# Nine conditioning pairs of a hybrid encoder summed on VectorE ahead of TensorE, with two more weight slots

## Chip, cores and metric

One core of one Trainium2 chip runs the whole kernel in one launch. The metric is the device time of that core in microseconds, the median of several executions. The reference's output, in float32, is what the kernel must produce.

## What is computed

Two groups of tokens, a prompt of 512 and a sample of 64, pass through a trunk of two layers at width 1024. Every layer takes a condition vector per group and turns it into 6 x 1024 values (a shift, a gain and a gate for each of two blocks):

```
mod = silu(c) @ ada_w[l] + ada_b[l]            # (2 groups, 6 * 1024)
sh1, sc1, g1, sh2, sc2, g2 = split(mod, 6)
xm = rms(x) * (1 + sc1) + sh1                  # first block's input
q, k, v, o, gates = split(xm @ w_in)           # mLSTM mixer of layer 0
...
x = x + g1 * (h @ w_out)                       # h from the matrix memory, gated by sigmoid(o)
xm = rms(x) * (1 + sc2) + sh2
x = x + g2 * swiglu(xm)
```

Layer 1 has differential attention in the mixer's place. The 6 x 1024 values of layer 0 are 48 units of 128; the first 16 (shift and gain of the first block) are needed at the very start, the other 32 (units 16 to 47) form 16 pairs, numbered 0 to 15. None of the pairs is needed before the gate and the second block of layer 0.

## The kernel before

Tensors lie feature by token: 8 tiles (k = 0 to 7) of 128 features by 576 tokens. A weight matrix is cut in units of 128 output features, one unit being 8 tiles of 128 x 128, that is 512 KB. SyncE's queue loads units in a fixed, written-out order into two raw slots (`load_unit`, L431); GpSimd splits each into a high and a low part (`split_unit`, L613 and L617) as soon as TensorE has left the slot's parts; TensorE multiplies high by high, high by low and low by high (`project`, L730: 48 matmuls of 288 columns a unit; `project_values`, L786: 28 matmuls of 512 columns a unit for V). The units of the mixer are the gates (0), Q (1 to 4), K (5 to 8), V (9 to 16), O (17 to 24) and the output matrix (25 to 32). The kernel calls a matvec of a conditioning pair `modulate(p)`. It stands in TensorE's instruction stream between units: one after unit 2 and one after each two units of Q and K (p = 0 to 3), one after each two units of V (p = 4 to 7), one inside the matrix-memory core at every odd head (p = 8 to 11) and one after each two units of the output matrix (p = 12 to 15).

A matvec (L741) has silu(c) spread over 32 columns as one operand and the pair's 256 weights a row as the other: 8 k tiles x 4 strips of 32 output rows, accumulated in PSUM. Its two units come through one slot, `ada_ring`, loaded by `load_ada` (L438) between the other loads, each waiting for the matvec before.

Layer 1's values and the late ones of layer 0 are already made in another way, in quads of four units while the FFN runs: VectorE multiplies the weights of one k tile by the condition's value per partition and adds them up over the eight k tiles (`quad_products`, L1844 and L1848, one chain in bank 4 and one in bank 5, the last step written to SBUF), and TensorE only sums the result over the partitions (`modulate_four`, L757).

While Q and K are projected, VectorE works on the gate rows of the mixer and waits for ScalarE and TensorE. TensorE then runs `columns` (L854 to L859, small transposes of these rows), and V. After each of the first five units of V it turns a tile of keys (`turn_keys`, L874), which VectorE weighs (`weigh_keys`, L2098) out of bank 6. After the fourth unit of V ScalarE and VectorE empty banks 0 to 4 (`mixer_values`, L1453 on ScalarE, L2059 and L2063 on VectorE) before TensorE can begin the fifth, since both halves use the same banks. VectorE then masks the decays (`mask`, L2107 and L2112), ScalarE exponentiates them.

Of the kernel before, what the change touches and what calls it, by code (L numbers as in the profile page):

```python
# [33 lines left out]
ALU = mybir.AluOpType  # L34
# [3 lines left out]
P = 128  # L38
D = 1024
KT = D // P  # L40
# [45 lines left out]
ADA_START = 16  # L86
ADA_QUADS = 48


# [60 lines left out]
def build(nc, x_in, cond, consts, small, oh_line, table, w_stream, w_down, ada_w, c0n_in, kcache, vcache,  # L150
          line_dram, y_out, cp_out, cs_out, m_out, k_out, vp_out, vs_out):
    with ExitStack() as ctx:
# [7 lines left out]
        def at(name, shape, offset, dt=F32):  # L160
            return nc.alloc_sbuf_tensor_at(name, shape, dt, offset=offset)
# [49 lines left out]
        kw = at("kw", [P, TT, H, DK], off + 8 * T * 4)  # L211
        vm = at("vm", [P, TT, H, 130], off + (8 * T + TT * H * DK) * 4)
        assert (8 * T + TT * H * (DK + 130)) * 4 <= 2 * FH * T * 4
# [82 lines left out]
        ada_first_in = [sem(f"ada_first_in{g}") for g in range(ADA_START // 2)]  # L296
        ada_in = [sem(f"ada_in{s}") for s in range(2)]
        first_mv, xm_ready, cs_zero, ada_mv = (sem(n) for n in ("first_mv", "xm_ready", "cs_zero", "ada_mv"))
        silu_ready, mod_ready = sem("silu_ready"), sem("mod_ready")
# [101 lines left out]
        first_rows = lambda g: psum[:, 6 + g % 2, 0:64]  # L401
        late_rows = [psum[:, 7, 258 + 64 * n:322 + 64 * n] for n in range(3)] + [psum[:, 4, 400:464]]
        pair_rows = lambda p: late_rows[p - 8] if 8 <= p < 12 else psum[:, 5, 64 * (p % 8):64 * (p % 8) + 64]
        quad_rows = psum[:, 6, 0:4 * 32]
# [20 lines left out]
        def _(sp):  # L425
# [7 lines left out]
            def load_ada(n0, i=0):  # L433

                p = (n0 - ADA_START) // 2
                if p >= 1:
                    sp.wait_ge(ada_mv, i + p)
                sp.dma_start(ada_ring[:, n0 % 2].rearrange("p k c -> p (k c)"), ada_w[i * 2 + n0]).then_inc(ada_in[n0 % 2], 16)  # L438

            def load_quad(q, parts):  # L440
# [35 lines left out]
            load_unit(2)  # L476
            load_ada(16)
            load_ada(17)
# [22 lines left out]
            load_pairs(U_O, 9, 30)  # L501

# [207 lines left out]
        def _(pe):  # L710
# [33 lines left out]
            def modulate(p):  # L744

                for half in range(2):
                    pe.wait_ge(ada_in[half], 16 * (p + 1))
# [11 lines left out]

            def project_values(u0, a, tails, ada0=None, between=None, free=None, banks=(range(TT), range(TT))):  # L760

                parts, pairs = act[BUF[a]], samples[tails // 2]
                for nh in range(2):
                    for kp in range(4):
                        u = u0 + 4 * nh + kp
                        s = u % 2
                        pe.wait_ge(lo_split, u + 1)
                        for kk in range(2):
                            k = 2 * kp + kk
                            for tt in range(TT):  # L770
                                t0 = tt * P
                                if nh == 0 and k == 0 and tt == 4:
# [16 lines left out]
                        if ada0 is not None and kp % 2 == 1:  # L789
                            modulate(ada0 + 2 * nh + kp // 2)  # L790
                        if between is not None:
                            between(4 * nh + kp)
# [69 lines left out]
            def turn_keys(tt):  # L862
# [12 lines left out]
                last.then_inc(ktr_ready, 1)  # L875

            columns()
            project_values(U_V, A_IN, 0, ada0=4, between=turn_keys)
            pe.wait_ge(v_tail, 2)
# [8 lines left out]
            def core_scores(p):  # L888

                q, k = ([qk[a * DK:(a + 1) * DK, n + p] for a in range(2)] for n in (0, 4))  # L890
                if p == 0:
                    pe.wait_ge(rows_turned, 1)
                pe.wait_ge(p_ready, 2 * p)
# [20 lines left out]
            def core_values(h):  # L914
# [174 lines left out]

            pe.wait_ge(groups_set, 2)  # L1090
            ffn(U_FFN0, A_FFN0, N_FFN0, 0)
# [266 lines left out]
        def _(sa):  # L1358
# [89 lines left out]
            def mixer_values(nh):  # L1448
                sa.wait_ge(unit_done, U_V + 4 * nh + 4)
                for tt in (0, 1, 4) if nh == 0 else (4, 0, 1):  # L1450
                    r = slice(0, P) if tt < 4 else slice(TS, P)
# [348 lines left out]
        def _(ve):  # L1800
# [12 lines left out]
            def modulation(n0, n1, done, norm=None):  # L1813
# [3 lines left out]
                ve.wait_ge(ada_mv, p + units // 2)  # L1817
                if p == 8:
                    for c, n, rows in ((0, 192, psum[:, 7, 258:450]), (192, 64, late_rows[3])):
                        steps(ve.transpose(cols[:, c:c + n], rows))  # L1820
                    steps.wait()
                else:
                    ve.transpose(cols, psum[:, 5, 64 * (p % 8):64 * (p % 8) + 32 * units]).then_inc(rows_turned, 1)
                    ve.wait_ge(rows_turned, 1 if p == 0 else 2)
                last = tt_(mod[:, n0:n1, :], by_unit(cols)[:, :, 0:2],
# [6 lines left out]
                ve.wait_ge(mod_ready, done)  # L1832

            def quad_products(q, k0, k1):

                if k0 == 0:
                    ve.wait_ge(quad_in[q % 2], 64 * (q // 2 + 1))
                done = 2 * KT * q
# [186 lines left out]
            ve.reduce_sum(lam4[:, 0:2], tmp[:, 4, 0:128].rearrange("p (a d) -> p a d", a=2), AX.X).then_inc(lam_dot, 1)  # L2025
            steps(ve.memset(vm[TS:P, 4], 0.0))
            steps.wait()
            ve.memset(vm[:, :, :, P:P + 1], 1.0).then_inc(vones, 1)


# [161 lines left out]

            modulation(16, 32, 1)
            for h in range(H + 1):
# [12 lines left out]
            ve.wait_ge(lo_ready[A_HN], H)  # L2207
            modulation(32, 40, 2, norm=(1, SH_B + 1))
            shift_lo(A_FFN0, SH_B)
# [475 lines left out]
```

## Time and profile before

| what | value |
|---|---|
| median of 3 runs | 1498.81 us (1498.41 to 1499.83) |
| the profiled execution | 1501.64 us, span 1499.8 us |
| granted TensorE clock, mean over the span | 0.998 |
| TensorE busy | 1464.8 us, 98% of the span |
| VectorE busy | 950.1 us, 63% |
| GpSimd busy | 758.1 us, 51% |
| ScalarE busy | 419.0 us, 28% |
| mean transfer rate | 122 GB/s |

The table's shares are means over the span; the profile also gives busy time by stretch, the order of instructions on every engine, what each wait ended on, and the chain of work that ended last. TensorE's matmuls overlap in the records: from one start to the next is less than the duration of one.

### The profile page before, as it was taken

To read this page: it belongs to the slowest core of one execution; us is meant where nothing else is said; L and a number is where in the kernel's file an instruction comes from. 1 tells how busy PE (TensorE), PEld (TensorE's weight loads), DVE (VectorE), ACT (ScalarE), POOL (GpSimd) and SP (SyncE) were. 2 spreads that over 40 slices of the span, in tenths; PEclk is the share of its full clock that TensorE was granted. 3 is DMA by queue.
4 is the path that set the end of the run, shared out by engine and by line. 5 is a ranking of instruction groups with operands and counts; after the bars stand their busy time and mean duration, and the time that the engine had idled before them with its cause. 6 is when DMAs were issued, how large, how long until landed. Compare 5 with 4: busy or idle time off the path is not lost.

```text
span 1499.8 us, 30413 instructions
## 1 busy us (share of the span) xinstructions
PE 1464.8 (98%) x11892; PEld 1382.7 (92%) x11892; DVE 950.1 (63%) x1713; ACT 419.0 (28%) x895; POOL 758.1 (51%) x512
## 2 busy tenths in 40 slices
PE   5999999999999999999999999999999999999999
PEld 4998898999999999999999777778999999999999
DVE  4503465457774367776676257776975778567688
ACT  4302454221110011113211146665321223111142
POOL 2445333555555455555444534465655555556554
PEclk9999999999999999999999999999999999999999
DMA  9455423444456344453322342220222222222222
GB/s 368 143 186 171 141 71 114 148 148 157 166 177 222 100 141 166 144 183 116 106 75 74 93 161 87 87 85 31 85 85 84 80 95 78 85 79 76 88 97 102
DMA packets 57536, 183.58 MB, mean 122 GB/s; under 512 B 6441, under 2 KB 9905, under 8 KB 57441
## 3 DMA queue, kind: packets, MB, share of 16 engines
q1 hardware_dynamic: 54528, 179.34, 35.8%
q10 hardware_dynamic: 2912, 2.92, 0.6%
q8 instruction: 65, 1.06, 0.3%
q14 instruction: 31, 0.25, 0.1%
HBM read 171.69 MB, written 10.55 MB: 122 GB/s over the span
## 4 chain that ended last, share of the span: by engine, by line
PE 85%; DVE 4%; POOL 3%; DMA 3%; issue 2%; ACT 2%; SPq 0%; ACTq 0%; POOLq 0%; DVEq 0%
PE psum L730 60%; PE psum L786 7%; PE psum L991 4%; PE psum L1188 2%; POOL w_sum L688 2%; DMA raw<-in_w_down 2%; PE psum L741 1%; DMA ada_first<-in_ada_w 1%; PE psum L1280 1%; PE psum L1124 1%; PE psum L1243 1%; PE psum L1103 1%; DVE act_lo L1901 1%; PE psum L1230 1%; PE psum L929 1%
## 5 line engine op out<-in xcount | busy, mean ns | idle before, releaser
L613 POOL TENSOR_SCALAR w_hi<-raw 128x1024 fp32r<-128x1024 f32 (+1 forms) x168 | 192.5, 1146 | 583.8 <-PE psum L730 490.0
L617 POOL TENSOR_TENSOR w_lo<-raw,w_hi 128x1024 fp32r<-128x1024 f32 (+2 forms) x195 | 437.4, 2249 | 14.0
L730 PE MATMUL psum<-act_hi,w_hi 128*128 128x288 f32 (+1 forms) x1952 | 426.4, 299 | 0.2
L730 PE MATMUL psum<-act_hi,w_lo 128*128 128x288 f32 (+1 forms) x1952 | 420.0, 297 | 0.0
L730 PE MATMUL psum<-act_lo,w_hi 128*128 128x288 f32 (+1 forms) x1952 | 420.0, 296 | 0.0
L730 PEld LDWEIGHTS psum<-act_hi,w_hi 128*128 128x128 f32 x1952 | 315.6, 189 | 6.5 <-issue 2.7
L730 PEld LDWEIGHTS psum<-act_hi,w_lo 128*128 128x128 f32 x1952 | 315.7, 189 | 0.0
L730 PEld LDWEIGHTS psum<-act_lo,w_hi 128*128 128x128 f32 x1952 | 315.3, 189 | 0.0
L730 PE MATMUL psum<-hid_both,w_hi 128*128 128x288 f32 x704 | 122.6, 296 | 0.0
L730 PEld LDWEIGHTS psum<-hid_both,w_hi 128*128 128x128 f32 x704 | 103.6, 189 | 0.8 <-issue 0.8
L1848 DVE SCALAR_TENSOR_TENSOR psum<-ada_quad,cst,psum 128x512 f32<-128x512 f32 x144 | 96.9, 749 | 0.0
L730 PE MATMUL psum<-hid_both,w_lo 128*128 128x288 f32 x352 | 75.4, 296 | 0.0
L991 PE MATMUL psum<-hid_both,w_ring 128*128 128x288 f32 x440 | 73.6, 294 | 0.0
L1556 ACT ACTIVATE hid_both<-tmp 128x576 f32 (+1 forms) x22 | 15.1, 686 | 198.5 <-DVE tmp L1951 198.5
L991 PE MATMUL psum<-mix_hi,w_ring 128*128 128x288 f32 x320 | 66.6, 295 | 1.8 <-DVE w_ring L2449 1.8
L1917 DVE SCALAR_TENSOR_TENSOR x<-psum,mod,x 128x288 f32<-128x288 f32 (+5 forms) x72 | 25.6, 411 | 67.3 <-PE psum L730 66.8
L2471 DVE SCALAR_TENSOR_TENSOR tmp<-tmp,tiny 128x512 f32<-128x512 f32 (+1 forms) x44 | 63.7, 1486 | 3.9 <-ACT tmp L1583 1.7
L991 PEld LDWEIGHTS psum<-hid_both,w_ring 128*128 128x128 f32 x440 | 63.6, 188 | 0.0
L730 PEld LDWEIGHTS psum<-hid_both,w_lo 128*128 128x128 f32 x352 | 56.7, 189 | 0.0
L1552 ACT ACTIVATE tmp<-tmp,tiny 128x512 f32<-128x512 f32 (+1 forms) x44 | 21.2, 528 | 124.0 <-DVE tmp L1940 124.0
L991 PEld LDWEIGHTS psum<-mix_hi,w_ring 128*128 128x128 f32 x320 | 52.2, 188 | 2.2 <-issue 2.2
L688 POOL TENSOR_TENSOR w_sum<-raw 128x640 f32<-128x640 f32 x16 | 29.2, 1826 | 47.3 <-DMA raw<-in_w_down 41.6
(365 smaller groups left out, 2393.3 us busy)
## 6 DMA issues: line engine op xcount, KB each, us to landing
raw<-in_w_stream SPq DMA_DIRECT2D x153, 512.0 KB, 3.5
ada_quad<-in_ada_w SPq DMA_DIRECT2D x48, 512.0 KB, 4.5
raw<-in_w_down SPq DMA_DIRECT2D x32, 704.0 KB, 4.3
ada_ring<-in_ada_w SPq DMA_DIRECT2D x32, 512.0 KB, 4.3
ada_first<-in_ada_w SPq DMA_DIRECT2D x8, 1024.0 KB, 14.2
line_rep<-line SPq DMA_DIRECT2D x8, 352.0 KB, 4.6
line<-line_rep SPq DMA_DIRECT2D x8, 352.0 KB, 5.3
x<-in_x SPq DMA_DIRECT2D x4, 576.0 KB, 5.6
```

What stands on the lines that cost most here:

```text
L613: pool.tensor_scalar(hi, src, 1.0, 0.0, ALU.mult, ALU.add).then_inc(hi_split, 1)
L617: last = pool.tensor_tensor(lo[:, c:c + w], src[:, c:c + w], hi[:, c:c + w].bitcast(F32), ALU.subtract)
L688: pool.tensor_tensor(w_block(d, name), w_block(d, a), w_block(d, b), op).then_inc(sum_ready, 1)
L730: last = mm(psum[:, b + half, 0:n_cols], weights[wp][:, k, :], parts[ap][:, k, half * HT:half * HT + n_cols], start=(k == 0 and n == 0), s ...
L786: last = mm(psum[:, banks[nh][tt], :], tokens, w, start=(k == 0 and n == 0), stop=(k == KT - 1 and n == len(products) - 1))
L991: last = mm(psum[:, bank, 0:HT], w_ring[:, (g + 2) % 4, wp, k, :], mixed(j, ap, k), start=(k == 0 and i == 0), stop=(stop and k == MK - 1 ...
L1188: last = mm(psum[:, 7, 0:n_cols], w_parts[u % 2][wp][:, j // 3, :], act[0][ap][:, j // 3, half * HT:half * HT + n_cols], start=(j == 0), s ...
L1552: last = af(tmp[:, 4, a0:a1], tmp[:, 2, a0:a1], ACT.Silu, bias=shift_sb[:, 0, g:g + 1])
L1556: af(hid[0][:, i, :], tmp[:, 5, :], ACT.Copy).then_inc(hhi_ready, 1)
L1848: last = stt(out=quad_acc[g] if k < KT - 1 else quad_sum[:, g], in0=w, scalar=c, in1=quad_acc[g], op0=ALU.mult, op1=ALU.add)
L1917: last = stt(out=xs, in0=psum[:, 2 * s + half, a0:a1], scalar=mod[:, i * 2 + (8 * c + j), g:g + 1], in1=xs, op0=ALU.mult, op1=ALU.add)
L2471: last = stt(out=h[:, a0:a1], in0=tmp[:, 3, a0:a1], scalar=shift_sb[:, 1, g:g + 1], in1=tmp[:, 4, a0:a1], op0=ALU.add, op1=ALU.mult)
```

## The change

Pairs 0 to 8 are made as the quads are: VectorE multiplies and adds over the eight k tiles (`pair_products`), 16 instructions of 128 x 256 a pair, both groups in bank 5 (columns 0 to 255 and 256 to 511), the last step of each written to SBUF; TensorE sums over partitions (`modulate_sum`). Each pair's weights go to one of three slots: `ada_ring` and two new ones in the place of the mixer's value tile `vm`, which is filled only after the fourth unit of V. So the two memsets of `vm` move behind the fourth key tile's wait, ScalarE's first filling of `vm` waits for pair 6's products, and the loads of the pairs (`load_pair`) wait for products, not for matvecs. TensorE's sums stand after the fourth and the sixth unit of Q and K counted from unit 3 (two each) and after V's units 0, 2, 3, 5 and 7. Pairs 9 to 15 stay matvecs; 9 to 11 take the places of 8 to 10 in the core, and the place at the last head is empty.

```diff
+SUM_PAIRS = 9
+PAIR_SLOT = (0, 1, 2, 0, 1, 2, 1, 0, 0)
+PAIR_SUM = (0, 1, 2, 0, 1, 2, 0, 0, 0)
...
+        ada_more = at("ada_more", [P, 2, 2, KT, P], vm_at)
+        sum_more = at("sum_more", [P, 2, 2, 2, P], vm_at + 4 * KT * P * 4)
...
+            def load_pair(p):
+                before = pair_before(PAIR_SLOT, p)
+                if before is not None:
+                    sp.wait_ge(pair_part, 2 * KT * (before + 1))
+                elif PAIR_SLOT[p]:
+                    sp.wait_ge(first_mv, 6)
+                for j in range(2):
+                    sp.dma_start(pair_tile(p)[:, j]..., ada_w[ADA_START + 2 * p + j])...
...
-            for u in (3, 4):
+            for u in range(3, 9):
                 load_unit(u)
-            load_pairs(5, 2, 18)
+                if u in (5, 6, 8):
+                    load_pair((5, 6, 8).index(u) + 1)
...
             for h in range(H):
                 load_unit(U_V + h)
-                load_ada(22 + h)
+                if h < 4 or h == 7:
+                    load_pair({0: 4, 1: 5, 2: 7, 3: 6, 7: 8}[h])
                 load_rows(h)
...
+            def modulate_sum(p):
+                pe.wait_ge(pair_part, 2 * KT * (p + 1))
+                rows, sums = pair_rows(p), pair_sum(p)
+                for g in range(2):
+                    for j in range(4):
+                        r = slice(32 * j, 32 * j + 32)
+                        last = mm(by_unit(rows[r]), group_cols[:, g, :], sums[:, g, :, r], start=(g == 0), stop=(g == 1))
+                last.then_inc(ada_mv, 1)
...
-            modulate(0)
             for p in range(1, 4):
                 project(U_Q + 2 * p, 0, act[0])
                 project(U_Q + 2 * p + 1, 0, act[0])
-                modulate(p)
+                if p >= 2:
+                    modulate_sum(2 * p - 4)
+                    modulate_sum(2 * p - 3)
...
+            def between_values(n):
+                turn_keys(n)
+                for p in {0: (4,), 2: (5,), 3: (6,), 5: (7,), 7: (8,)}.get(n, ()):
+                    modulate_sum(p)
...
-                if h % 2 == 1:
-                    modulate(8 + h // 2)
+                    pe.wait_ge(rows_turned, 1)
+                if h % 2 == 1 and h < 7:
+                    modulate(9 + h // 2)
...
+            def pair_products(p, k0=0, k1=KT):
+                ...
+                for k in range(k0, k1):
+                    for g in range(2):
+                        w, c = pair_tile(p)[:, :, k, :], cs_col(k)[:, g:g + 1]
+                        ve.wait_ge(pair_part, done + (2 * k - 1 + g if k else 0))
+                        if k == 0:
+                            last = ts_(pair_acc[:, g], w, c, None, ALU.mult)
+                        else:
+                            if k == KT - 1 and g == 0 and before is not None:
+                                ve.wait_ge(ada_mv, before + 1)
+                            last = stt(out=pair_acc[:, g] if k < KT - 1 else pair_sum(p)[:, g], in0=w, scalar=c, in1=pair_acc[:, g],
+                                       op0=ALU.mult, op1=ALU.add)
+                        last.then_inc(pair_part, 1)
...
+            pair_products(0)
             ve.wait_ge(floor_ready, 1)
...
+            for p in range(1, 4):
+                pair_products(p)
+            pair_products(4, 0, 6)
             ve.wait_ge(acol_mm, 1)
...
-            for tt in range(3):
-                weigh_keys(tt)
+            pair_products(4, 6)
+            pair_products(5, 0, 5)
+            weigh_keys(0)
+            pair_products(5, 5)
+            pair_products(6, 0, 4)
+            weigh_keys(1)
+            pair_products(6, 4)
+            pair_products(7, 0, 3)
+            weigh_keys(2)
+            ve.wait_ge(ada_mv, 6)
+            steps(ve.memset(vm[TS:P, 4], 0.0))
+            steps.wait()
+            ve.memset(vm[:, :, :, P:P + 1], 1.0).then_inc(vones, 1)
+            pair_products(7, 3, 7)
             mixer_values(0)
+            pair_products(7, 7)
             for tt in range(3, TT):
                 weigh_keys(tt)
             mask(0)
             mask(1)
+            pair_products(8)
             mixer_values(1)
```

## Rows read from the trace of the kernel before

**Rows 1.** The page, busy time, share of the span and instructions of an engine.

```profile
PE 1464.8 (98%) x11892; PEld 1382.7 (92%) x11892; DVE 950.1 (63%) x1713; ACT 419.0 (28%) x895; POOL 758.1 (51%) x512
```

**Rows 2.** The chain that ended last, 0 to 420 us: start us, length us, what.

```profile
54.25 1.03 PE psum L741 x64
...
156.85 1.29 DVE vm L2059 x2
...
246.80 0.65 ACT tmp L1517
...
252.21 1.39 ACT tmp L1485 x10
```

**Rows 3.** Timeline of TensorE around the matvec of pair 2: start us, length us.

```profile
81.84 0.42 PE L730 MATMUL psum<-act_hi,w_lo 128*128 128x288 f32 x2
82.19 0.99 PE L741 MATMUL psum<-ada_ring,cst 128*32 128x64 f32 x56
...
83.22 0.53 PE L730 MATMUL psum<-act_hi,w_hi 128*128 128x288 f32 x2
83.59 0.43 PE L730 MATMUL psum<-act_lo,w_hi 128*128 128x288 f32 x2
...
95.84 0.42 PE L730 MATMUL psum<-act_hi,w_lo 128*128 128x288 f32 x2
96.19 0.99 PE L741 MATMUL psum<-ada_ring,cst 128*32 128x64 f32 x56
```

**Rows 4.** Timeline of TensorE around a quad's sum over partitions.

```profile
374.43 0.65 PE L757 MATMUL psum<-quad_sum,group_cols 128*32 128x128 f32 x16
375.06 0.53 PE L730 MATMUL psum<-act_hi,w_hi 128*128 128x288 f32 x2
```

**Rows 5.** Timeline of TensorE in V, units 1, 4 and 7.

```profile
111.98 0.40 PE L786 MATMUL psum<-w_lo,samples 128*128 128x512 f32 x1
112.31 0.99 PE L741 MATMUL psum<-ada_ring,cst 128*32 128x64 f32 x56
...
113.34 0.66 PE L874 MATMUL psum<-cst,qk 128*128 128x128 f32 x4
...
128.82 0.48 PE L786 MATMUL psum<-w_hi,act_hi 128*128 128x512 f32 x1
...
150.09 0.45 PE L786 MATMUL psum<-w_hi,act_hi 128*128 128x512 f32 x1
```

**Rows 6.** Timeline of ScalarE at the end of V's fourth unit.

```profile
127.48 1.71 ACT L1453 ACTIVATE vm<-psum 128x512 f32<-128x512 f32 x3 [27.53 <-PE psum L786]
```

**Rows 7.** Timeline of GpSimd, the split of the last unit of V.

```profile
142.70 4.80 POOL L613 TENSOR_SCALAR w_hi<-raw 128x1024 fp32r<-128x1024 f32 x1 [3.09 <-PE psum L786]
147.59 2.40 POOL L617 TENSOR_TENSOR w_lo<-raw,w_hi 128x1024 fp32r<-128x1024 f32 x1
```

**Rows 8.** Timeline of VectorE in a quad's products, 0.66 us from start to start.

```profile
332.92 1.41 DVE L1844 TENSOR_SCALAR psum<-ada_quad,cst 128x512 f32<-128x512 f32 x2 [2.64 <-DMA ada_quad<-in_ada_w]
334.24 4.04 DVE L1848 SCALAR_TENSOR_TENSOR psum<-ada_quad,cst,psum 128x512 f32<-128x512 f32 x6
```

**Rows 9.** Groups by line and shape, VectorE, 0 to 420 us: busy us, mean ns.

```profile
L1848 DVE SCALAR_TENSOR_TENSOR psum<-ada_quad,cst,psum 128x512 f32<-128x512 f32 x42 | 28.3, 749 | 0.0
...
L2168 DVE SCALAR_TENSOR_TENSOR cs_sb<-c0n,tmp,psum 64x129 f32<-64x129 f32 x8 | 2.8, 349 | 0.3
```

**Rows 10.** Timeline of VectorE, 62 to 164 us.

```profile
62.16 0.14 DVE L2070 TENSOR_SCALAR tiny<-sml 128x1 f32<-128x1 f32 x1
70.05 0.09 DVE L2073 MEMSET tmp<- 128x40 f32 x1 [7.75 <-ACT tmp L1442]
...
72.27 0.14 DVE L2081 COPY tmp<-long_rows 8x1 f32<-8x1 f32 x1
98.80 0.19 DVE L2085 COPY tiny<-psum 128x32 f32<-128x32 f32 x1 [26.39 <-PE psum L859]
...
136.65 4.72 DVE L2107 TENSOR_TENSOR dec<-dec,cst 128x512 f32<-128x512 f32 x4
...
145.44 1.14 DVE L2112 TENSOR_TENSOR qw<-qw,qk 128x448 f32<-128x448 f32 x2
...
163.09 0.73 DVE L2168 SCALAR_TENSOR_TENSOR cs_sb<-c0n,tmp,psum 64x129 f32<-64x129 f32 x2
```

**Rows 11.** Timeline of SyncE's queue, the load of V's fourth unit.

```profile
99.98 0.34 SPq L431 DMA_DIRECT2D raw<-in_w_stream  x1
```

More of the change, by code:

```diff
@@ L211, in build @@
         kw = at("kw", [P, TT, H, DK], off + 8 * T * 4)
-        vm = at("vm", [P, TT, H, 130], off + (8 * T + TT * H * DK) * 4)
+        vm_at = off + (8 * T + TT * H * DK) * 4
+        vm = at("vm", [P, TT, H, 130], vm_at)
+        ada_more = at("ada_more", [P, 2, 2, KT, P], vm_at)
+        sum_more = at("sum_more", [P, 2, 2, 2, P], vm_at + 4 * KT * P * 4)
+        assert (4 * KT + 8) * P <= TT * H * 130
         assert (8 * T + TT * H * (DK + 130)) * 4 <= 2 * FH * T * 4
@@ L401, in build @@
         first_rows = lambda g: psum[:, 6 + g % 2, 0:64]
-        late_rows = [psum[:, 7, 258 + 64 * n:322 + 64 * n] for n in range(3)] + [psum[:, 4, 400:464]]
-        pair_rows = lambda p: late_rows[p - 8] if 8 <= p < 12 else psum[:, 5, 64 * (p % 8):64 * (p % 8) + 64]
+        late_rows = [psum[:, 7, 258 + 64 * n:322 + 64 * n] for n in range(3)]
+        pair_rows = lambda p: late_rows[p - 9] if 9 <= p < 12 else psum[:, 7 if p < 8 else 6 if p == 8 else 5, 64 * (p % 8):64 * (p % 8) + 64]
+        pair_tile = lambda p: ada_more[:, PAIR_SLOT[p] - 1] if PAIR_SLOT[p] else ada_ring[:, :, :, :]
+        pair_sum = lambda p: sum_more[:, PAIR_SUM[p] - 1] if PAIR_SUM[p] else rstd[:, 0:512].rearrange("p (g u c) -> p g u c", g=2, u=2)
+        pair_acc = psum[:, 5, :].rearrange("p (g u c) -> p g u c", g=2, u=2)
+        pair_before = lambda uses, p: max((q for q in range(p) if uses[q] == uses[p]), default=None)
         quad_rows = psum[:, 6, 0:4 * 32]
@@ L476, in _ @@
             load_unit(2)
-            load_ada(16)
-            load_ada(17)
+            load_pair(0)
             for a in range(2):
@@ L498, in _ @@
                 load_unit(U_V + h)
-                load_ada(22 + h)
+                if h < 4 or h == 7:
+                    load_pair({0: 4, 1: 5, 2: 7, 3: 6, 7: 8}[h])
                 load_rows(h)
-            load_pairs(U_O, 9, 30)
+            load_pairs(U_O, 1)
+            load_pairs(U_O + 2, 7, 34)
+            load_pairs(U_O + 16, 1)
             def load_four(u0, q):
@@ L746, in modulate @@
                 for half in range(2):
-                    pe.wait_ge(ada_in[half], 16 * (p + 1))
+                    pe.wait_ge(ada_in[half], 16 * (p + 1 - SUM_PAIRS + PAIR_SLOT.count(0)))
                 matvec(pair_rows(p), lambda k: ada_ring[:, :, k, :], ada_mv)
+            def modulate_sum(p):
[6 more added lines that the diff above has]
+                last.then_inc(ada_mv, 1)
             def modulate_four(q, i=0):
@@ L758, in modulate_four, with project_values @@
                 last.then_inc(quad_mv, 1)
-            def project_values(u0, a, tails, ada0=None, between=None, free=None, banks=(range(TT), range(TT))):
+            def project_values(u0, a, tails, between=None, free=None, banks=(range(TT), range(TT))):
                 parts, pairs = act[BUF[a]], samples[tails // 2]
@@ L788, in project_values @@
                         last.then_inc(unit_done, 1)
-                        if ada0 is not None and kp % 2 == 1:
-                            modulate(ada0 + 2 * nh + kp // 2)
                         if between is not None:
@@ L875, in turn_keys @@
                 last.then_inc(ktr_ready, 1)
+            def between_values(n):
+                turn_keys(n)
+                for p in {0: (4,), 2: (5,), 3: (6,), 5: (7,), 7: (8,)}.get(n, ()):
+                    modulate_sum(p)
             columns()
-            project_values(U_V, A_IN, 0, ada0=4, between=turn_keys)
+            project_values(U_V, A_IN, 0, between=between_values)
             pe.wait_ge(v_tail, 2)
@@ L1449, in mixer_values @@
                 sa.wait_ge(unit_done, U_V + 4 * nh + 4)
+                if nh == 0:
+                    sa.wait_ge(pair_part, 2 * KT * 7)
                 for tt in (0, 1, 4) if nh == 0 else (4, 0, 1):
@@ L1817, in modulation @@
                 ve.wait_ge(ada_mv, p + units // 2)
-                if p == 8:
-                    for c, n, rows in ((0, 192, psum[:, 7, 258:450]), (192, 64, late_rows[3])):
-                        steps(ve.transpose(cols[:, c:c + n], rows))
+                if p == 0:
+                    ve.transpose(cols[:, 0:512], psum[:, 7, :])
+                    ve.transpose(cols[:, 512:576], pair_rows(8)).then_inc(rows_turned, 1)
+                    ve.wait_ge(rows_turned, 1)
+                elif p == 9:
+                    steps(ve.transpose(cols, psum[:, 7, 258:450]))
                     steps.wait()
@@ L1832, in modulation @@
                 ve.wait_ge(mod_ready, done)
+            def pair_products(p, k0=0, k1=KT):
+                if k0 == 0:
+                    turn = PAIR_SLOT[:p].count(PAIR_SLOT[p]) + 1
+                    if PAIR_SLOT[p]:
+                        ve.wait_ge(quad_in[PAIR_SLOT[p] - 1], 32 * turn)
+                    else:
+                        for half in range(2):
+                            ve.wait_ge(ada_in[half], 16 * turn)
+                done, before = 2 * KT * p, pair_before(PAIR_SUM, p)
+                for k in range(k0, k1):
[4 more added lines that the diff above has]
+                            last = ts_(pair_acc[:, g], w, c, None, ALU.mult)
+                        else:
+                            if k == KT - 1 and g == 0 and before is not None:
[3 more added lines that the diff above has]
+                        last.then_inc(pair_part, 1)
             def quad_products(q, k0, k1):
                 if k0 == 0:
-                    ve.wait_ge(quad_in[q % 2], 64 * (q // 2 + 1))
+                    ve.wait_ge(quad_in[q % 2], 32 * PAIR_SLOT.count(1 + q % 2) + 64 * (q // 2 + 1))
                 done = 2 * KT * q
```

16 lines of the change are left out of this document (7 added, 9 removed).

## The prediction

> **What bounds the kernel.** I began with busy time by engine: TensorE is busy 98% of the span [rows 1]. That alone doesn't say that each of its microseconds counts, so I read the chain that ended last next. Between 54 and 420 us it is nearly all TensorE, and the matvecs lie on it in their own right: 1.03 us for the one of pair 0, for instance [rows 2]. It leaves TensorE at two places that matter here. After V's last unit it goes over VectorE's emptying at 156.85, so what TensorE does there (matvec 7) is hidden. At the last head it goes over ScalarE from 246.80 to the squares at 252.21, and the matvec of that head, 1.03 us of TensorE right after 246.80, is hidden too [rows 2]. Then I read TensorE's timeline for what a matvec takes, and those of VectorE, ScalarE and GpSimd for what stands ready when TensorE comes earlier.
>
> **Matvecs removed.** Matmuls of L730 come in twos, and from 83.59 to 95.84 there are 46 steps, 0.266 us each. Around the matvec it is 83.59 - 81.84 = 1.75 us over what would be two steps, 0.53 us. A matvec between two units so costs 1.21 us [rows 3]; 1.03 us is its own, 0.18 us entry and exit. Matvecs 0, 1 and 2 give 3.63 us. Matvec 3 is followed by the small transposes, not by a unit, and I take 0.08 + 1.03 = 1.11 us. In V the matvec takes 113.34 - 112.31 = 1.03 us, and 0.10 us more to enter (0.33 us from 111.98, where matmuls of L786 follow one another by 0.23 us) [rows 5]: 1.13 us for matvec 4. Matvecs 5 and 6 are taken up below. Matvec 7 and that of the last head give 0.
>
> **Sums added.** The trace has no sum of this size. A quad's, of 16 records of 128 columns, takes 375.06 - 374.43 = 0.63 us [rows 4], and that is the upper bound. The pair's has 16 records of 64 columns, a quarter of a matvec's 64. The matvec's 56 and 8 records take 1.03 us start to start, and its strips of 64 columns 0.0145 us each (0.81 us to 56 of them), so 48 fewer leave 1.03 - 0.70 = 0.33 us; below this, 16 x 0.0145 = 0.23 us is the floor. I take 0.33 us for a first sum, being nearest in width, 0.23 us for the second of two, 0.18 us entry and exit among units of L730 and 0.07 us in V. Each of the two places in Q and K pays 0.33 + 0.23 + 0.18 = 0.74 us (0.64 at the second, before the transposes).
> Q and K: 3.63 + 1.11 - 0.74 - 0.64 = 3.36 us saved. V's units 0 to 3: 1.13 - 0.40 (sum 4) - 0.40 (sum 5) = 0.33 us.
>
> **Two places where the saving stops.** Before V's fifth unit stands matvec 5 with sum 6 in its place, but TensorE there also needs ScalarE's first two of three copies: 127.48 + 2/3 x 1.71 = 128.62 [rows 6], where it began at 128.82 [rows 5]. The matvec covered this wait. Less start-up, 0.12 us is left of the 0.8 us. Before V's last unit matvec 6 covered another one: GpSimd's split of that unit ended at 147.59 + 2.40 = 149.99 [rows 7], and the unit began at 150.09 [rows 5]. The split starts when V's sixth unit ends, and its first step took 4.80 us against 1.05 us elsewhere because VectorE's masks, 136.65 to 146.58 [rows 10], held it up. Masks and split keep their places relative to TensorE's key turning and units, so matvec 6 saves 0.06 us. Sum: 3.36 + 0.33 + 0.12 + 0.06 = 3.9 us. Nothing behind 157 us changes on the chain: three matvecs stay in the core, the transposing of the first rows gains a second instruction on VectorE under the first unit of O, and the wait for it moves to the first head's values, 6 us behind it.
>
> **VectorE's products** are hidden if they are on time. There are 9 x 16 = 144 of 128 x 256. None is in the trace. The quads' products of 512 columns take 0.749 us and start 0.66 us apart ((4.04 - 0.75) / 5) [rows 8, 9]; one of 129 columns takes 0.349 us [rows 9], so a column costs 1.04 ns, and 256 fewer leave 0.48 us of duration and 0.39 us from start to start. I take 0.39 us: the lower bound. The upper one is from the row where such instructions do not overlap at all, 0.38 us apart at 0.349 us of duration [rows 9, 10]: 0.51 us.
> At 0.39 us a pair is 6.3 us. Pair 0 runs from 62.3 [rows 10], when its weights have long been there (matvec 0 ran at 54.25 [rows 2]), to 68.6. The floor rows come at 70.05 - 1.21 = 68.8 and take 2.35 us as before, to 71.2. Pairs 1, 2, 3 end at 77.5, 83.8, 90.1, the first three quarters of pair 4 at 94.8. TensorE asks for pair 1 at 82.19 - 2.42 + 0.33 = 80.1, for pair 3 at 96.19 - 3.63 + 0.74 + 0.33 = 93.6 [rows 3], and hands over the columns at 98.80 - 3.36 = 95.4. Each is met, with 2.6, 3.5 and 0.6 us to spare. After 1.2 us for the columns come 50 products, three weighings of 0.7 us and the memsets (1.0 us): 22.6 us from 96.6, some 2.6 us more for waits on TensorE's turns, to 121.8. VectorE's emptying must start by 1.3 us after V's fourth unit (127.44 - 3.7 + 1.3 = 125.0). The masks then end at 142.7, pair 8 at 149.0, V at 152.9. So VectorE is nowhere last, by 3 us in the main stretches.
>
> **Loads.** SyncE's queue moves the same bytes. A pair's two transfers now stand together and wait for the products of the slot's last pair, with rows and the next unit queued behind them. The closest is pair 6, which waits for pair 4 (98.2), right behind V's fourth unit, at 99.98 - 3.4 [rows 11]: a wait of 1.5 us in the queue. The next unit behind it can't start before GpSimd's next split anyway, some 9 us later. Cost 0; cover gone only if products are 7 us late.
>
> **A rule against it.** From start to start the quads' products leave 0.09 us less than their duration [rows 8, 9]: they overlap. The Trainium skill, "VectorE: DVE Perf Modes", section "The DRAIN you can't avoid", says that the next operation doesn't start until the pipeline is empty. By that rule the pair products would be their full duration apart. The rows of the quads speak against it, though those alternate between two banks.
>
> **Rivals.** With later products, the first loss is at pair 3 (48 products behind 71.2: from 0.46 us each), the second at the emptying.
> (a) Products one after the other, 0.48 us: pair 0 ends at 70.0, the floor rows at 72.4, pair 3 at 95.4, with TensorE waiting 1.5 us; pair 4 is late by 0.4 us; the emptying starts at 129.5 where TensorE, by then at 126.6, allows no more: 2.9 us. 4.8 - 3.9: 0.9 us slower, 1499.7.
> (b) Slower: one bank is the mechanism. Each product reads and writes the bank into which the one before still writes, and is held until that is done, 0.51 us apart. Pair 3 then ends at 97.3 (3.7 us late), pair 4 0.6 us late, the emptying 3.8 us late: 8.1 - 3.9 = 4.2 us slower, 1503.0. By the same steps it decides from 0.475 us on, and passes 0.2% at 0.50. Against it: inside one quad product reading and writing one bank cost nothing visible.
> (c) A sum costs as a quad's: six on the path at 0.3 us more, 1.8 us: 1496.7. For it: 16 records each. Against it: half the columns.
> (d) The masks hold up GpSimd less, since VectorE's order around them moves: 0.6 us more saved, 1494.3.
>
> **Numbers.** Forecast 0.62, (a) 0.08, (b) 0.08, (c) or a wait of that size elsewhere 0.16, (d) 0.06. Time: 1498.81 - 3.9 = 1494.9 us. The sum was made in a profiled execution of 1501.64 us, 1.8 us outside its span and 2.8 us above the median; 3.9 us is taken off either. 0.2% (3.0 us) is what counts as a difference. Range 1493.5 (all of (d), floor price of the sums) to 1499.0 (all of (c), the lighter part of (a)); (b), half of (a) and tails lie outside, under 2 in 10. Faster 0.58: most of the forecast, which is only 0.9 us past the bound, and (d). Same 0.33: (a), (c), the forecast's rest. Slower 0.09: (b).
>
> **What would show it.** Matvecs of L741 fall from 1536 records (512 first, 1024 of the ring) by 576. The product rows should read 0.48 us, 0.39 us apart, with pair 3 done before TensorE's second two sums. V's fourth unit should end 3.7 us earlier, and V's last unit should stand behind GpSimd's low part with a TensorE wait of 0.6 us. The prediction is wrong if TensorE's waits name VectorE's products or emptying, which is (a) or (b), or if the sums take over 0.6 us.

## The result and the profile after

The changed kernel takes 1510.51 us (median of 6 executions, 1505.78 to 1515.03) against 1498.61 us before (6 executions, 1497.41 to 1499.83): ratio 1.0077, interval 1.0059 to 1.0094. It is 11.9 us slower where 3.9 us less was forecast, and lies outside the range. The profiled execution took 1509.32 us with a span of 1507.5 us.

Line numbers have moved: L730 is L758, L741 is L769, L786 is L824, L613 and L617 are L641 and L645. The new products are L1896 and L1900, the new sums L785. Busy time, share and instructions by engine, from the page of the changed kernel, against [rows 1]:

```profile
PE 1461.5 (97%) x11460; PEld 1380.1 (92%) x11460; DVE 1011.6 (67%) x1857; ACT 418.9 (28%) x895; POOL 757.4 (50%) x512
```

TensorE has 432 matmuls and 3.3 us of work fewer, VectorE 61.5 us more. The span is 7.7 us longer, so TensorE stands still or runs slower somewhere. The chain that ended last, of the changed kernel (start us, length us, what), to the end of V:

```profile
123.46 1.09 ACT vm L1497 x2
...
138.56 4.80 POOL w_hi L641
143.44 2.40 POOL w_lo L645
145.89 6.76 PE psum L824 x28
152.68 1.29 DVE vm L2125 x2
```

V's emptying starts at 152.68 where it started at 156.85 [rows 2]: 4.2 us earlier, 0.3 us more than the forecast's 3.9. This execution is the best of its kind: in the five other profiled executions with the same work up to there (further down) the emptying starts at 153.24 to 153.75, 3.1 to 3.6 us earlier. From VectorE's last small instructions ahead of pair 0's products (L2135, at 62.15 here) to the emptying it is 90.5 us in all six, so the 0.6 to 1.1 us that the five lack arise before any product runs; they were not traced further. The chain names both places where the saving was to stop, ScalarE's copies and GpSimd's split, and no product of VectorE. TensorE's sums in its timeline:

```profile
79.14 0.43 PE L785 MATMUL psum<-rstd,group_cols 128*32 128x64 f32 x16
79.38 0.41 PE L785 MATMUL psum<-sum_more,group_cols 128*32 128x64 f32 x16
79.72 0.53 PE L758 MATMUL psum<-act_hi,w_hi 128*128 128x288 f32 x2
...
124.69 0.47 PE L824 MATMUL psum<-w_hi,act_hi 128*128 128x512 f32 x1 [0.47 <-ACT vm L1497]
...
145.89 0.50 PE L824 MATMUL psum<-w_hi,act_hi 128*128 128x512 f32 x1 [0.45 <-POOL w_lo L645]
```

Two sums take 0.24 + 0.34 = 0.58 us where the forecast had 0.56. The products, in VectorE's timeline:

```profile
71.33 4.79 DVE L1900 SCALAR_TENSOR_TENSOR psum<-ada_more,cst,psum 128x256 f32<-128x256 f32 x12
...
88.96 0.87 DVE L1900 SCALAR_TENSOR_TENSOR rstd<-ada_ring,cs_last,psum 128x256 f32<-128x256 f32 x2
...
147.84 0.85 DVE L1900 SCALAR_TENSOR_TENSOR rstd<-ada_ring,cs_last,psum 128x256 f32<-128x256 f32 x2
```

Twelve in 4.79 us with 0.48 us for one is 0.39 us from start to start. Pair 3 is ready at 89.8, pair 8 at 148.7. So far the forecast holds. The loss is in the output stage. The chain of the same trace there:

```profile
261.50 1.07 PE psum L769 x64
...
262.73 0.33 SPq L452
...
263.26 4.33 DMA raw<-in_w_stream
...
267.85 1.05 POOL w_hi L641
...
268.99 2.35 POOL w_lo L645
...
271.38 6.69 PE psum L758 x48
```

It reads: matvec 12 ends at 262.57; SyncE's queue, which had waited for it, issues half a pair (L452), then the load of unit 28; the load lands 4.3 us later, GpSimd splits it in 3.5 us, TensorE begins it. The same pattern comes at 279 and 299. TensorE's timeline at the three units, then its windows (columns: TensorE, weight loads, VectorE, ScalarE, GpSimd busy us; granted clock; DMA share; GB/s):

```profile
271.38 0.53 PE L758 MATMUL psum<-act_hi,w_hi 128*128 128x288 f32 x2 [2.26 <-POOL w_lo L645]
...
289.10 0.85 PE L758 MATMUL psum<-act_hi,w_hi 128*128 128x288 f32 x2 [3.40 <-POOL w_lo L645]
...
310.25 0.85 PE L758 MATMUL psum<-act_hi,w_hi 128*128 128x288 f32 x2 [4.43 <-POOL w_lo L645]
```

```profile
271.00:278.00 7.00, 6.62 (x48) 6.46 (x48) 4.25 (x3) 1.32 (x3) 4.08 (x3) 1.00 0.00 0
...
289.00:298.00 9.00, 8.90 (x48) 8.85 (x48) 2.23 (x3) 0.00 (x0) 4.38 (x3) 0.69 0.00 0
...
310.00:319.00 9.00, 8.74 (x52) 8.59 (x56) 2.39 (x3) 0.00 (x0) 4.54 (x3) 0.72 0.40 118
```

The waits make 10.1 us. Behind the second and the third the granted clock is at its lower level, 1.2 GHz, for some 5 us, and the unit takes 9.1 and 8.8 us instead of the 6.7 us of the one behind the first wait. The chains have matvec 15 at these places, in the changed kernel and in the kernel before:

```profile
319.02 1.03 PE psum L769 x64
```

```profile
307.90 1.03 PE psum L741 x64
```

It is 11.1 us later, from 4.2 us earlier at V's end. The 15.3 us between are 10.1 us of waits, 2.4 and 2.1 us of lower clock, and some 0.8 us around the waits (behind the first, at full clock, it is 16.58 us from one matvec to the next: 2.26 us of wait, the 14.05 us of before and 0.27 us more). At the end only 7.7 us are left. The profiled execution of the kernel before lost 2.5 us of busy TensorE more from 1200 to 1320 us, in the last FFN (116.6 us busy of 120, 119.1 in the changed kernel's); the remaining 0.9 us I did not trace. The medians of six executions each lie 11.9 us apart, 15.6 us over the forecast.

Why the queue waits can be read off four lines of the diff, which are not among those shown with the change:

```diff
-            load_pairs(U_O, 9, 30)
+            load_pairs(U_O, 1)
+            load_pairs(U_O + 2, 7, 34)
+            load_pairs(U_O + 16, 1)
```

`load_pairs(U_O + 2, 7, 34)` puts pair 9 beside units 19 and 20, and so pair 13 beside units 27 and 28. The load of each half waits for the matvec of the pair before it. Matvec 12 stands behind unit 26, so the half of pair 13 between the loads of units 27 and 28 holds back unit 28 until unit 26 is finished. Before, pair 12 stood there, whose wait was for the last head's matvec, 19 us ahead of matvec 12 (246.8 against 265.7). SyncE's queue in the kernel before, from the first half of pair 12, issued when that matvec had ended, to the load of unit 28:

```profile
248.00 0.33 SPq L438 DMA_DIRECT2D ada_ring<-in_ada_w  x1
251.06 0.33 SPq L431 DMA_DIRECT2D raw<-in_w_stream  x1
```

Unit 28's load is issued at 251.06 there, and behind 263 us in the changed kernel.

### The profile page after: what moved, and what is told of

It is laid out like the page before. It is cut to its first block, busy times and chain, and to the rows that moved or that the text cites. A ratio compares the mean times of both kernels' runs of the same rounds, so it can differ in the third digit from the quotient of the medians.

```text
span 1507.5 us, 29649 instructions
## 1 busy us (share of the span) xinstructions
PE 1461.5 (97%) x11460; PEld 1380.1 (92%) x11460; DVE 1011.6 (67%) x1857; ACT 418.9 (28%) x895; POOL 757.4 (50%) x512
## 4 chain that ended last, share of the span: by engine, by line
PE 86%; DVE 5%; issue 2%; DMA 2%; ACT 2%; POOL 2%; SPq 1%; ACTq 0%; POOLq 0%; DVEq 0%
PE psum L758 59%; PE psum L1034 7%; PE psum L824 7%; PE psum L1230 2%; DMA ada_first<-in_ada_w 1%; PE psum L1322 1%; DMA raw<-in_w_stream 1%; PE psum L1166 1%; PE psum L769 1%; PE psum L1040 1%; POOL w_lo L645 1%; PE psum L1285 1%; PE psum L1145 1%; POOL w_hi L641 1%; DVE act_lo L1971 1%
## 5 line engine op out<-in xcount | busy, mean ns | idle before, releaser
L641 POOL TENSOR_SCALAR w_hi<-raw 128x1024 fp32r<-128x1024 f32 (+1 forms) x168 | 193.2, 1150 | 595.5 <-PE psum L758 469.4
L645 POOL TENSOR_TENSOR w_lo<-raw,w_hi 128x1024 fp32r<-128x1024 f32 (+2 forms) x195 | 438.1, 2252 | 14.0
L758 PE MATMUL psum<-act_hi,w_hi 128*128 128x288 f32 (+1 forms) x1952 | 428.3, 301 | 11.2 <-POOL w_lo L645 10.1
L758 PE MATMUL psum<-act_lo,w_hi 128*128 128x288 f32 (+1 forms) x1952 | 421.3, 297 | 0.0
L758 PE MATMUL psum<-act_hi,w_lo 128*128 128x288 f32 (+1 forms) x1952 | 421.3, 297 | 0.0
L758 PEld LDWEIGHTS psum<-act_hi,w_hi 128*128 128x128 f32 x1952 | 317.3, 190 | 17.8 <-POOL w_lo L645 10.8
L758 PEld LDWEIGHTS psum<-act_hi,w_lo 128*128 128x128 f32 x1952 | 316.9, 190 | 0.0
L758 PEld LDWEIGHTS psum<-act_lo,w_hi 128*128 128x128 f32 x1952 | 316.8, 190 | 0.0
L758 PE MATMUL psum<-hid_both,w_hi 128*128 128x288 f32 x704 | 122.7, 296 | 0.0
L758 PEld LDWEIGHTS psum<-hid_both,w_hi 128*128 128x128 f32 x704 | 103.6, 189 | 0.8 <-issue 0.8
L758 PE MATMUL psum<-hid_both,w_lo 128*128 128x288 f32 x352 | 75.4, 296 | 0.0
L758 PEld LDWEIGHTS psum<-hid_both,w_lo 128*128 128x128 f32 x352 | 56.7, 189 | 0.0
L824 PE MATMUL psum<-w_hi,act_hi 128*128 128x512 f32 x128 | 51.7, 404 | 0.9 <-ACT vm L1497 0.5
```

Source lines behind the costliest of these rows:

```text
L641: pool.tensor_scalar(hi, src, 1.0, 0.0, ALU.mult, ALU.add).then_inc(hi_split, 1)
L645: last = pool.tensor_tensor(lo[:, c:c + w], src[:, c:c + w], hi[:, c:c + w].bitcast(F32), ALU.subtract)
L758: last = mm(psum[:, b + half, 0:n_cols], weights[wp][:, k, :], parts[ap][:, k, half * HT:half * HT + n_cols], start=(k == 0 and n == 0), s ...
L824: last = mm(psum[:, banks[nh][tt], :], tokens, w, start=(k == 0 and n == 0), stop=(k == KT - 1 and n == len(products) - 1))
```

## The experiments

All ratios are to the kernel before, on the same chip.

**The order mended.** The one edit in the changed kernel:

```diff
-            load_pairs(U_O + 2, 7, 34)
-            load_pairs(U_O + 16, 1)
+            load_pairs(U_O + 2, 3, 34)
+            load_pairs(U_O + 8, 1)
+            load_pairs(U_O + 10, 4, 40)
```

> The changed kernel with one edit in SyncE's queue: pairs 12 to 15 are loaded again beside units 27 to 34, as before the change, so that no load of a unit stands behind a wait for the matvec that follows the unit before it. Theory Q (queue): the whole loss is the queue of the output stage. V's end stays 4.2 us ahead of the kernel before, TensorE has no wait for GpSimd's split between 262 and 310 us, the granted clock there is 1.00, and the time is 4.2 us under the kernel before: 1494.4, ratio 0.9972. Rival W (VectorE's extra 62 us of work slows TensorE or its clock somewhere): the time stays over the kernel before, and stretches with a clock under 1.00 remain although TensorE has no gap.

Measured: 1495.79 us (12 executions), ratio 0.9974 (0.9963 to 0.9984). TensorE is busy all of the output stage, at full clock:

```profile
262.00:310.00 48.00, 48.00 (x580) 46.98 (x579) 24.14 (x43) 11.18 (x22) 25.11 (x15) 1.00 0.44 143
```

Undoing the order takes away the loss, and all of VectorE's work is still there: rival W falls. The ratio's 3.9 us is the forecast's size, the medians of this chip differ by 2.5 us; 4.2 us lies in the interval. V's emptying started at 153.58, only 3.3 us ahead of the kernel before, not 4.2.

**The blocks alone, in the kernel before.** Pair halves ahead, then a wait for the matvec:

```diff
-            load_pairs(U_O, 9, 30)
+            load_pairs(U_O, 5, 30)
+            for n in range(4):
+                u = U_O + 10 + 2 * n
+                load_unit(u)
+                load_ada(40 + 2 * n)
+                load_ada(41 + 2 * n)
+                if n in (0, 1, 2):
+                    sp.wait_ge(ada_mv, 13 + n)
+                load_unit(u + 1)
```

> The kernel before with the blocking alone: both halves of a pair are loaded behind units 27, 29 and 31, and units 28, 30 and 32 then wait in the queue for matvecs 12, 13 and 14. No sums on VectorE. Theory Q: TensorE waits 2.3, 3.4 and 4.4 us for GpSimd's splits, the clock falls behind the second and third, and matvec 15 ends 15.4 us later than in the kernel before (324.4 instead of 309.0): time 1498.8 + 12 to 16 = 1511 to 1515. Rival W: TensorE waits 10 us in all but the clock stays at 1.00, so at most +10: 1509 or less.

Measured: 1503.17 us, ratio 1.0028 (1.0017 to 1.0038). The direction is right, the size is a third of what I expected. TensorE's waits:

```profile
276.32 0.54 PE L738 MATMUL psum<-act_hi,w_hi 128*128 128x288 f32 x2 [1.26 <-POOL w_lo L625]
...
291.49 0.53 PE L738 MATMUL psum<-act_hi,w_hi 128*128 128x288 f32 x2 [0.85 <-POOL w_lo L625]
...
306.85 0.53 PE L738 MATMUL psum<-act_hi,w_hi 128*128 128x288 f32 x2 [1.04 <-POOL w_lo L625]
```

They are 1 us each and no unit behind them is slow. So the wait for the matvec alone does not make the loss of the changed kernel. Of the 4.9 us between the medians the three waits explain 3.1; in the profiled execution 1.5 us more went at the last head, where the granted clock fell (0.83 from 252 to 262 us).

**One block** (`n in (0,)` in the same edit).

> The kernel before with the first of the three blocks alone (unit 28 waits for matvec 12). Theory Q: one TensorE wait of 2.3 us, no fall of the clock behind it, and the later units catch nothing up: +2.3 us, 1501.1, ratio 1.0015. Rival (the three waits are one chain that would arise anyway once the queue is late): the waits before units 30 and 32 come too, some 10 us.

Measured: 1500.27 us, ratio 1.0008 (0.9997 to 1.0019). One TensorE wait of 1.11 us where 2.3 was expected, none at units 30 and 32. Each block stands for itself; by time alone this can't be told from no change.

**The exact queue of the changed kernel, in the kernel before.**

```diff
-            load_pairs(U_O, 9, 30)
+            load_pairs(U_O, 5, 30)
+            load_unit(U_O + 10)
+            load_ada(40)
+            load_ada(41)
+            for n in range(3):
+                load_ada(42 + 2 * n)
+                load_unit(U_O + 11 + 2 * n)
+                load_ada(43 + 2 * n)
+                load_unit(U_O + 12 + 2 * n)
+            load_unit(U_O + 17)
```

> The kernel before with the queue of the output stage exactly as in the changed kernel: behind matvecs 12, 13 and 14 comes first one half of the next pair (512 KB), then unit 28, 30 or 32, then the other half and the next unit. e2_before_three_blocks had the unit and the next one first, and its TensorE waits were 1.3, 0.9 and 1.0 us instead of 2.3, 3.4 and 4.4, with no fall of the clock behind them. Theory R (the half pair ahead of the unit and the one behind it make the unit land late, and waits of over 3 us bring the clock down): waits of 2 to 4.5 us as in the changed kernel, the granted clock between 285 and 310 us under 0.9, matvec 15 15 us later than before, time 1498.3 + 11 to 16: 1510 to 1514. Rival S (the long waits and the clock are owed to the sums' version in some other way): the waits stay near 1 us as in e2, the clock at 1.00, time 1503.

Measured: 1510.15 us, ratio 1.0079 (1.0066 to 1.0092). With no product on VectorE the order of the queue costs 11.5 us between the medians. The changed kernel is as slow, but it had gained some 3 to 4 us by V's end; against its own mended order it loses 14.7 us. So the order alone, put into the kernel before, makes most of that loss and not all of it. The waits are 3.03, 2.10 and 2.05 us, and the clock falls behind the first. With 512 KB ahead of the unit and 1 MB behind it, it landed 4.4 to 5.4 us after its issue (4.3 to 6.5 in the changed kernel), against 3.5 to 4.0 us in the run with the three blocks, with nothing ahead and 1.5 MB behind. Theory R holds in kind. Its sizes do not: the waits make 7.2 us, not 10.1, and one unit of the output stage is slow (8.1 us), not two.

**The changed kernel again**, beside the last one and the next.

> The changed kernel itself, unedited, on the same chip as the other two. Both theories: 1.0077 of the kernel before as first measured, 1508 to 1512, with the three waits and the lower clock.

Measured: 1510.48 us, ratio 1.0074 (1.0055 to 1.0093); waits of 2.54, 3.61 and 3.88 us.

**Both units ahead of both halves**, the pairs left one group early:

```diff
-            load_pairs(U_O + 2, 7, 34)
+            load_pairs(U_O + 2, 3, 34)
+            for n in range(4):
+                for j in range(2):
+                    load_unit(U_O + 8 + 2 * n + j)
+                for j in range(2):
+                    load_ada(40 + 2 * n + j)
```

> The changed kernel with its pairs 12 to 15 loaded beside the same units as in it, but both units ahead of both halves, so that no unit's load stands behind the wait for a matvec but the one that GpSimd can't take yet. Theory R: the place inside the group is all, TensorE has no wait between 262 and 310 us, clock 1.00, time as e1_order_mended: 0.9974 of the kernel before. Rival (loading a pair one group early is itself harmful, because the next unit's load then waits for the matvec all the same): units 29 and 31 are late instead, waits of 1 us or more at them, time over 1500.

Measured: 1495.54 us, ratio 0.9977 (0.9968 to 0.9987), no TensorE wait from 262 to 310. Here it is unit 29 whose load stands behind the wait for matvec 12: it is issued at 265.46 and needed at 278.64, one unit later than unit 28, and nothing waits. The early pair does no harm by itself; that the unit needed next stands between its halves, behind the wait, does.

**The queue written out instead of looped**, in the changed kernel (`load_unit(U_O + 2 + n)` and `load_ada(34 + n)` for 14 values of n).

> The changed kernel with SyncE's loop over units 19 to 32 and pairs 9 to 15 written out, same order. In the changed kernel the first half of the pair is issued 0.2 us after the matvec and the unit's load 0.53 us behind it; in e5_before_exact_queue, written out there, 0.38 us. TensorE's waits were 10.1 us in the one and 7.2 us in the other. Theory L (the loop's slower issue makes the difference): waits fall to 7 to 8 us and the time to 1505 or 1506. Rival D (the transfers land later or earlier by themselves, 4.3 to 6.8 us after issue in both kernels): waits stay between 7 and 11 us and the time between 1505 and 1512, without relation to the loop; a change of the wait by under 1 us speaks for D.

Measured: 1510.29 us (4 executions), ratio 1.0073 (1.0056 to 1.009). The waits are 2.18, 2.88 and 3.97 us, 9.0 us in all, 1.1 us less than the changed kernel's 10.1, just over the 1 us that was to speak for rival D. The time did not move: all four executions took over 1509 us, so theory L's 1505 or 1506 fails. What makes 10.1 us of 7.2 stays open. The clock fell behind all three waits here, the one of 2.18 us among them: the unit behind it takes 8.2 us, and from its fourth line on two matmuls take 0.48 us instead of 0.27.

```profile
275.06 0.53 PE L760 MATMUL psum<-act_hi,w_hi 128*128 128x288 f32 x2 [2.18 <-POOL w_lo L647]
...
276.42 0.68 PE L760 MATMUL psum<-act_lo,w_hi 128*128 128x288 f32 x2
276.90 0.68 PE L760 MATMUL psum<-act_hi,w_lo 128*128 128x288 f32 x2
```

**TensorE kept busy in the waits**: in the changed kernel, ahead of units 28, 30 and 32:

```diff
+                for n in range(24):
+                    mm(psum[:, 4, 0:HT], act[1][0][:, n % 8, 0:P], act[1][0][:, (n + 1) % 8, 0:HT], start=True, stop=True)
```

> The changed kernel with 24 matmuls of 288 columns, 3.2 us, on TensorE between units 27 and 28, 29 and 30, 31 and 32, in the time in which it waits for the split; their results go to an idle bank and are used by nothing. Theory K (the clock falls because TensorE stands still for 3.4 us and more, and costs 2.6 us each time): the waits shrink to under 1.5 us, the granted clock between 262 and 320 us stays 1.00, no unit has matmuls 0.48 us apart by twos, and the time falls by 3 to 5 us against the changed kernel although TensorE does 9.6 us more: 1505.5 to 1507.5. Rival N (the clock falls for another reason, the low load of the memory or of the other engines): it falls again, and the time stays or rises, 1510 or more.

Measured: 1506.18 us, ratio 1.0045 (1.0031 to 1.006): 4.1 us under the unrolled kernel's 1510.29 on the same chip, where the slowest filled execution (1507.80) is faster than the fastest unfilled one (1509.87), and 4.3 us under the changed kernel's 1510.48 on another, with three times 3.3 us more of matmuls. The timeline has one wait left, and the window is at full clock:

```profile
270.08 3.34 PE L1010 MATMUL psum<-act_hi 128*128 128x288 f32 x24
...
291.83 0.53 PE L758 MATMUL psum<-act_hi,w_hi 128*128 128x288 f32 x2 [1.18 <-POOL w_lo L645]
```

```profile
262.00:322.00 60.00, 58.82 (x660) 57.56 (x659) 25.26 (x47) 10.77 (x21) 25.60 (x14) 1.00 0.36 130
```

The changed kernel has 0.89 over the same stretch. All five filled executions have a mean clock of 0.998 or 0.999; of the 16 of the changed and the unrolled kernel 15 have 0.990 to 0.995. Theory K holds for these waits: the clock falls because TensorE stands still. The Trainium skill, "TensorE: Matmul & The Clock Gate", section "HAM oscillation — how this bites in real kernels", describes it for waits on transfers between groups of matmuls; the traces agree that the clock falls behind such waits, which cost the unit behind it 2.4 and 2.1 us in the changed kernel.

**The first mask ahead of the last key tile**, on top of the mended order:

```diff
-            for tt in range(3, TT):
-                weigh_keys(tt)
-            mask(0)
+            weigh_keys(3)
+            mask(0)
+            weigh_keys(4)
             mask(1)
```

> e1_order_mended with one more edit on VectorE: the first mask runs ahead of the last key tile, in the 4.6 us in which VectorE waits for that tile, so that VectorE's masks end some 4 us earlier. Theory M (GpSimd's split of V's last unit is held up by the masks, 4.80 us where 1.05 us is usual, and TensorE waits for it): the first step of that split falls towards 1 to 2 us, TensorE's wait of 0.5 to 0.9 us ahead of V's last unit goes, time 0.6 us under e1: 1493.8. Rival P (the split is late for its load, or the masks then hold up the split of the unit before instead): the wait stays or moves one unit ahead, and the time is that of e1.

Measured: 1494.85 us, ratio 0.9969 (0.9959 to 0.9978). The split of V's last unit, against [rows 7]:

```profile
138.71 1.29 POOL L642 TENSOR_SCALAR w_hi<-raw 128x1024 fp32r<-128x1024 f32 x1 [3.40 <-PE psum L825]
```

1.29 us instead of 4.80, and TensorE has no wait ahead of that unit. From the start of this split to V's end it is 13.4 us, with the mended order alone 14.1: 0.7 us, at the place where it was expected. The medians differ by 0.9 us, but the intervals overlap, and the time is 1.1 us over the 1493.8 that was expected.

**The last head filled.** In the mended kernels the clock was below full once more, at 252 to 262 us, behind a TensorE wait of 2.73 us for ScalarE's scaled rows of the last head. In the kernel before this wait was 1.52 us. The clock fell behind it there in four of the seven profiled executions with 2.73 us, and in two of the four of the kernel before and its versions with 1.52 to 1.71 us. On top of the last version, 16 matmuls of 288 columns ahead of the turn (`for n in range(16): mm(psum[:, 4, 0:HT], act[0][0]...)`).

> e4_mended_mask_early with 16 matmuls of 288 columns (2.1 us) on TensorE ahead of the last head's turn, where it waits 2.7 us for ScalarE's scaled rows; their results are used by nothing. In the kernel before this wait was 1.5 us, since the last head's matvec stood there. Theory K (a wait of TensorE brings its clock down in a part of the executions, here after 252 us, where the granted clock was 0.83 in three of the profiled executions of changed kernels and 1.00 in others): the wait shrinks to 0.6 us, the clock behind it is 1.00, the spread of the times shrinks and the median falls by 1 to 1.5 us under e4: 1493.5. Rival (the clock there has nothing to do with the wait): the time is e4's, 1494.9, or a few tenths over it.

Measured: 1493.94 us, ratio 0.9971 (0.9962 to 0.998). The wait is 0.62 us, the window 252 to 262 has clock 1.00. Eight of 11 executions lie under 1494.5, three of 11 without the filling (on another chip), but three others reach 1495.8 to 1498.0, so the spread did not shrink, and the two ratios can't be told apart. The same with 8 matmuls in the kernel before:

> The kernel before with 8 such matmuls (1.1 us) at the same place, where it waits 1.5 to 1.7 us. Theory K: the wait shrinks to 0.5 us, and since the clock fell behind it in a part of the executions of this kernel's kin too (0.83 in two), the median falls by 0 to 1 us: 1497.5 to 1498.5. Rival: no change, or 0.2 us more.

Measured: 1498.55 us, ratio 1.0000 (0.9991 to 1.0009): no gain there. Of all versions those with the mended order and the early mask are the best, 0.3% under the kernel before.

## Why the prediction was wrong

**The step that failed** is "Nothing behind 157 us changes on the chain", with "Cost 0" for the loads. I weighed only those loads whose waits had become waits for products. Pairs 9 to 15 kept their kind of wait, so I took their order as unchanged, but nine pairs had gone out of the stream and the matvecs had moved up by one place (9 to 11 for 8 to 10) while the loads moved up by one group too, and those of pairs 12 to 15 had no reason to. For each wait in the queue the question was: which matvec does it name, and behind which unit does that one stand? For unit 28 that gives 26, two units ahead, and 0.7 + 4.3 + 3.8 us of issue, landing and split against 6.6 us of unit 27, the 2.3 us that TensorE waited. That the unit comes late could be summed from the trace of before. How much it costs could not: there the loads of units between 160 and 330 us land 3.6 us after their issue (median), which gives 0.7 + 3.6 + 3.8 - 6.6 = 1.5 us a unit and 4.5 us for three, some 0.6 us more than the saving. The later landings, up to 6.5 us, and the fall of the clock stood in no row that I had. None of my four rivals had the step at all. In its place the runs showed: 15.3 us lost in the profiled execution, 14.7 us between the medians of the changed kernel and the mended one, all undone by the order alone.

**Matvecs and sums**: right in kind and size. V's end came 4.2 us earlier in the first profiled execution and 3.1 to 3.6 us in five others, against 3.9; that the first came out so near owes something to luck. Two sums took 0.58 us against 0.56. Rival (c) falls.

**The two places where the saving stops**: right. TensorE's waits there are 0.47 and 0.45 us, and moving a mask gave the second back.

**VectorE's products**: right, 0.39 us apart at 0.48 us of duration, though both halves lie in one bank. Rivals (a) and (b) fall. The sum of (a) had a slip: pair 3 at 95.4 against 93.6, when TensorE asks, is a wait of 1.8 us, not 1.5, so (a) should have read 1500.0. The rule on draining, as the prediction has it, is not borne out by these rows either: the products start 0.09 us before the one ahead ends, as the quads' do. The same section of the Trainium skill adds that an operation that is not held starts earlier, so these rows speak against the rule as I used it and not against what the Trainium skill says. Rival (d) did not come by itself; the mask moved on purpose showed that its 0.6 us exists.

**The last head's matvec**, "gives 0", was right only by the chain. Its removal lengthens a wait of TensorE from 1.5 to 2.7 us, and in four of seven profiled executions the clock fell behind it. In the profiled execution of the mended order seven steps of two matmuls each, from 254.25 to 257.60, take 0.48 us instead of 0.27, about 1.5 us. This was not settled by time: filling the wait moved the median by 0.9 us within overlapping intervals.

**What would have made it right**: with the two mended orders 1495.79 and 1495.54 us were measured against 1494.9 forecast. By the medians of the same chip that is 2.5 and 3.1 us gained, against 3.9.

## What to carry to other kernels

When instructions leave a stream that another queue paces itself by, list every later wait of that queue again: which instruction it now names, what stands behind it in the queue, and how long issue, transfer and preparation take against the work that is still ahead of the engine. Keep transfers that must not wait out from between transfers that may. And a TensorE wait of a few microseconds has to be priced with the clock behind it: here 2.4 us on top of 3.4.

## What the runs showed of the hardware

- Products that read and write one PSUM bank in turn overlap as those in two banks do: 0.39 us from start to start at 0.48 us of duration, against 0.66 at 0.75 us.
- A 512 KB load landed 4.3 to 6.5 us after its issue with 0.5 MB just ahead and 1 MB behind it in the queue, 3.5 to 4.0 us with nothing ahead and 1.5 MB behind. That this spread makes the spread of the changed kernel's times, 1505.8 to 1515.0 us, is not shown. The mean clock over the span was 0.998 in the fastest of the six executions and 0.991 in the slowest.
- In the output stage the granted clock fell to the lower level behind TensorE waits of 2.18, 2.88, 3.03, 3.40, 3.61, 3.88, 3.97 and 4.43 us, not behind 0.85 to 1.26, 2.05, 2.10, 2.26 and 2.54 us. At the last head it fell behind 1.61 us, and behind 1.71 and 2.73 us in some executions and not in others, so the length of the wait alone does not decide it. With the waits filled by idle matmuls it stayed at 1.00.
- GpSimd's first step of a split takes 4.80 us beside VectorE's masks, which read two tensors in SBUF, and 1.29 us when these end 0.4 us after its start; beside the products, which read one there and one in PSUM, it stayed at 1.05 us.
